# An eighth pair of split buffers in a float32 transformer kernel, and one more weight subunit ahead of the second half of the tokens

## The reference, cut to what matters

```python
for l in range(2):                                             # first_block
    h = h + 0.5 * rms_norm(swiglu(rms_norm(h, g[0]), ffn1_w_in[l], ffn1_w_out[l]), g[1])
    h = h + rms_norm(mixer(rms_norm(h, g[2])), g[3])           # even: attention and conv, odd: GLA
    h = h + 0.5 * rms_norm(swiglu(rms_norm(h, g[4]), ffn2_w_in[l], ffn2_w_out[l]), g[5])
mod = silu(c) @ w_ada + b_ada                                  # second_block: shifts, scales, gates
h = rms_norm(x, norm1_w) * (1 + scale1) + shift1
proj = h @ w_in                                                # 15 chunks of columns
x = x + gate1 * ((sigmoid(ga) * y_attention + sigmoid(gb) * y_retention) @ w_out)
h2 = rms_norm(x, norm2_w) * (1 + scale2) + shift2
x = x + gate2 * ((silu(h2 @ w_gate) * (h2 @ w_up)) @ w_down)
out = rms_norm(x, final_norm_w)
```

## Time and profile before

| | |
|---|---|
| median of 3 runs | 1436.91 us (1436.34 to 1437.31) |
| the profiled execution: its own time | 1435.01 us |
| its span, first to last instruction | 1433.2 us |
| mean granted TensorE clock over the span | 0.998 |
| PE busy | 1415.5 us of the span |
| DVE busy, ACT busy | 947.2 us, 719.7 us |

### The profile page before, as it was taken

The page is one execution under the profiler, slowest core; times in us unless marked ns, Lnnn a source line. Parts: engine busy times, 40 slices in busy tenths (PEclk is TensorE's granted clock), DMA queues, the critical chain, the costliest instruction groups (busy, mean ns, idle before and its releaser), DMA issues.

```text
span 1433.2 us, 18097 instructions
## 1 busy us (share of the span) xinstructions
PE 1415.5 (99%) x6819; PEld 1164.5 (81%) x6819; DVE 947.2 (66%) x1321; ACT 719.7 (50%) x1063; POOL 149.9 (10%) x237
## 2 busy tenths in 40 slices
PE   9999999999999999999999999999999999999997
PEld 7888888688888888888887888887877788788886
DVE  6666667877675667576796857755568566655543
ACT  6444465565443454444754635446556644654442
POOL 1600010010000000000261100001452110100000
PEclk9999999999999999999999999999999999999999
DMA  9586765167776777776643678873945355565551
GB/s 319 191 249 210 245 226 192 53 191 219 222 263 214 228 254 231 237 261 202 210 147 128 205 178 262 270 220 112 248 149 191 120 174 176 162 206 178 188 206 60
DMA packets 236342, 286.51 MB, mean 200 GB/s; under 512 B 37028, under 2 KB 160464, under 8 KB 236256
## 3 DMA queue, kind: packets, MB, share of 16 engines
q1 hardware_dynamic: 235856, 284.99, 62.4%
q10 hardware_dynamic: 400, 0.38, 0.1%
HBM read 281.13 MB, written 4.20 MB: 199 GB/s over the span
## 4 chain that ended last, share of the span: by engine, by line
PE 91%; DVE 4%; ACT 2%; issue 1%; DMA 1%; POOL 0%; POOLq 0%; ACTq 0%; DVEq 0%
PE ps L580 28%; PE ps L583 28%; PE ps L581 27%; PE ps L915 2%; DVE wlo L472 1%; DMA raw<-in_w_in_dram 1%; PE ps L776 1%; PE ps L1474 1%; PE ps L1175 1%; ACT whi L463 1%; PE ps L1122 0%; DVE h L1917 0%; DVE ps L1914 0%; PE ps L553 0%; PE ps L1059 0%
## 5 line engine op out<-in xcount | busy, mean ns | idle before, releaser
L472 DVE TENSOR_TENSOR wlo<-raw,whi 128x1024 fp32r<-128x1024 f32 (+2 forms) x474 | 564.9, 1225 | 248.6 <-ACT whi L463 248.2
L463 ACT ACTIVATE whi<-raw 128x1024 fp32r<-128x1024 f32 (+2 forms) x474 | 472.0, 1042 | 246.7 <-PE ps L583 94.0
L580 PE MATMUL ps<-whi,xh 128*128 128x512 f32 (+2 forms) x1438 | 566.3, 394 | 2.7 <-DVE wlo L472 1.7
L581 PE MATMUL ps<-wlo,xh 128*128 128x512 f32 (+2 forms) x1438 | 553.8, 385 | 0.0
L583 PE MATMUL ps<-whi,xl 128*128 128x512 f32 (+2 forms) x1438 | 545.9, 386 | 0.0
L580 PEld LDWEIGHTS ps<-whi,xh 128*128 128x128 f32 x1438 | 270.2, 188 | 60.6 <-DVE wlo L472 4.1
L583 PEld LDWEIGHTS ps<-whi,xl 128*128 128x128 f32 x1438 | 269.9, 188 | 55.2
L581 PEld LDWEIGHTS ps<-wlo,xh 128*128 128x128 f32 x1438 | 270.4, 188 | 50.6
L580 PE MATMUL ps<-whi,gh 128*128 128x512 f32 x440 | 172.6, 392 | 0.0
L581 PE MATMUL ps<-wlo,gh 128*128 128x512 f32 x440 | 171.3, 389 | 0.0
L583 PE MATMUL ps<-whi,gl 128*128 128x512 f32 x440 | 153.5, 389 | 0.0
(11 more groups left out here) (256 smaller groups left out, 900.0 us busy)
## 6 DMA issues: line engine op xcount, KB each, us to landing
raw<-in_ffn_w_in_dram SPq DMA_DIRECT2D x174, 512.0 KB, 5.5
raw<-in_ffn_w_out_dram SPq DMA_DIRECT2D x40, 1024.0 KB, 5.9
raw<-in_w_in_dram SPq DMA_DIRECT2D x26, 1024.0 KB, 5.1
adat<-in_w_ada_dram SPq DMA_DIRECT2D x96, 256.0 KB, 2.9
raw<-in_w_ffn_gate_dram SPq DMA_DIRECT2D x22, 512.0 KB, 4.0
raw<-in_w_ffn_up_dram SPq DMA_DIRECT2D x22, 512.0 KB, 5.1
raw<-in_hyb_w_in_dram SPq DMA_DIRECT2D x10, 1024.0 KB, 5.4
raw<-in_gla_w_in_dram SPq DMA_DIRECT2D x10, 1024.0 KB, 5.3
```

The costliest lines, as they stand in the source:

```text
L463: e.activation(split_of(whi, j), raw_of(j), ACT.Copy).then_inc(*whi_made.up(j))
L472: e.tensor_tensor(split_of(wlo, j), raw_of(j), split_of(whi, j).bitcast(F32), ALU.subtract).then_inc(*wlo_made.up(j))
L580: e.matmul(ps[:, 0:n], a, whi_of(j, k), start=first and k == 0, stop=False)
L581: last = e.matmul(ps[:, 0:n], a, wlo_of(j, k), start=False, stop=False)
```

## The change

The ring of split pairs gets an eighth slot, and the memory for it comes from buffers that are laid over others. `lrT` and `wg` (GLA's small gate operands, 16 partitions) now lie in `xtmp`; in stage 6 `pT` lies in the modulation's `adat`, `rt` in `adaacc`, `iw` and `ik2` in `fold`. The load of `wg` moves from unit 4 of stage 4 to behind unit 6, with a wait on `xlo_made`; ACT's copy to `lrT` gets a wait on `xlo_made`. `lead` grows by one in every stage but 0, and the calls that place the splits move with it. `LOOK` and `LAG` stay, and the place of the transposes of half 1 in `first_order`'s loop stays.

```diff
-NSPL = 7
+NSPL = 8
...
-            lead = {6: 7, 7: 7}.get(st, 6)
+            lead = {6: 8, 7: 8}.get(st, 7)
...
             act_h_squares(e, st, 0)
-            split_hi(e, j0 + 6)
+            split_hi(e, j0 + 7)
             act_enter(e, st, 1)
...
             split_lo(e, j0 + 6)
-            dve_enter(e, st, 1)
+            for q in range(2):
+                dve_gain(e, st, 1, q)
+            split_lo(e, j0 + 7)
+            for q in range(2):
+                dve_xlo(e, st, 1, q, xtmp_of(q))
             first(0)
...
                         e.wait_ge(*lr_turned.at())
+                        e.wait_ge(*xlo_made.at(4, 1, 1))
                         e.activation(lrT[:, :], tb.of("lr")[0:16, 0:256], ACT.Copy).then_inc(*lr_made.up())
...
             act_hn(e, st, 1)
+            split_hi(e, j0 + 8)
             act_ada_x(e, st, 1)
...
-            dve_ada_x(e, st, 1, lambda: split_lo(e, j0 + 7))
+            dve_ada_x(e, st, 1, lambda: split_lo(e, j0 + 8))
...
-                        e.wait_ge(*h_made.at(4, 1, 1))
-                        e.dma_start(wg[:, :], T["gla_w_gate"][0]).then_inc(*s_wg.up())
...
+                if u == U0[4] + 6:
+                    e.wait_ge(*xlo_made.at(4, 1, 0))
+                    e.dma_start(wg[:, :], T["gla_w_gate"][0]).then_inc(*s_wg.up())
```

More of the change, by code:

```diff
@@ L148, in program @@
         xtmp = sb("xtmp", 1024)
+        wg, lrT = xtmp[0:16, 0:512], xtmp[0:16, 512:768]
         mhalf = sb("mhalf", P)[:, 0:8]
@@ L413, in program @@
             lr = sb("glr", 32, where=inner)
-            lrT = sb("glrT", 256, where=inner, parts=16)
-            wg = sb("gwg", 512, where=inner, parts=16)
         with ExitStack() as inner:
@@ L418, in program @@
             AL = sb("AL", 1024, F32R, where=inner)
-            ar = sb("ar2", 13712, where=inner)
+            ar = sb("ar2", 11776, where=inner)
         def x_view(z, q, tok):
@@ L1969, in program @@
         sga, sgb = A(2048, 0), A(2048, 2048)
-        MB = A(384)
-        SCW = off[0]
-        SC, W = A(384), A(384)
+        MB, SC, W = A(384), A(384), A(384)
         PB = [SC, W, iqT[:, 0:384], iqT[:, 384:768]]
-        pT = [A(384), A(384)]
-        off[0] = SCW + 1536
-        RSb = A(1536, SCW)
+        off[0] = 4096 + 1536
+        RSb = A(1536, 4096)
         qrT, krT, vr, sgr = A(1024), A(1024), A(2048), A(2048)
-        rt = A(512)
         decay = hid[1][:, :]
-        iw, ik2 = A(16), A(256)
-        assert off[0] <= 13712, off[0]
+        assert off[0] == 11776, off[0]
+        pT = [adat[0][:, 0:384], adat[1][:, 0:384]]
+        rt = adaacc
+        iw, ik2 = fold[:, 0:16], fold[:, 256:512]
         MJ = {name: J0[6] + 4 * i for i, name in enumerate(
```

## The result

| | before | after |
|---|---|---|
| median | 1435.73 us (21 runs, 1434.86 to 1437.31) | 1438.24 us (21 runs, 1436.52 to 1442.29) |
| the profiled execution: own time, span | 1435.01, 1433.2 us | 1437.46, 1435.7 us |

The ratio of after to before is 1.0016, with a 95% interval from 1.0010 to 1.0022: 2.3 us slower (1.4 to 3.2). The forecast was 1.6 us. The two traces differ by 2.5 us of span, all of it in waits of PE.

What follows compares the result with a forecast made beforehand. PE, busy 1415.5 of 1433.2 us, was taken as the bound, so only its waits could change. Losses of 0.4 (stage 2), 0.3 (stage 4) and 0.9 (stage 6) make 1.6 us on 1436.91: 1438.5 us, range 1434.7 to 1441.6.

Steps and rivals of the forecast that it cites:

- no difference by 0.2%: Whole kernel: time changes by less than about 0.2%, which is 2.9 us; given a chance of 0.73.
- Stage 2, forecast 0.4: Opening of stage 2: a fifth split ahead of the residual starts it 1.8 us later; a loss of 0.4 us.
- Stage 4, forecast 0.3: Stage 4, narrow subunits: PE reaches (6, 0) before its `wlo` is ready; a loss of 0.3 us.
- Stage 1, forecast 0: Stage 1: `wlo` 6, made behind DVE's two L800, counted as ready when PE comes to (6, 0); 0 us.
- behind wider matmuls: Feed-forward stages and stage 1: PE comes to (6, 0) later, behind wider matmuls, so its `wlo` is ready; no loss.
- Stage 6, forecast 0.9: Inside stage 6: later half 1 delays casts, splits and loads, so PE's wait at L2398 grows from 0.9 to 1.8 us.
- so is every link: Stage 6: with (3, 1) 0.9 us later, every link of the chain to L2030 is 0.9 us later too.
- Rival C: Stage 6: the gate write also slows the load before it, landing 7.7 us late; 4.7 us slower, 1441.6 us; chance 0.16.
- The openings of stages 6 and 7, forecast 0: Openings of stages 6 and 7: PE's waits stand ahead of (0, 1), so the longer lead changes nothing; 0 us.
- list of waits at the openings: Openings of stages 2, 6 and 7: six waits of PE, 4.8 us in all.
- waits for PE there: Ends of most stages: DVE and ACT wait for PE, so one more split before the residual is free.
- Rival A: Stage openings: earlier splits shrink PE's waits by 2.0 or 4.8 us, to 1434.9 or 1432.1 us; chance 0.12.

Runs made afterwards that it cites:

- experiment 1: The change with `ahead` stopping one split earlier at the ends of stages, as before; eight slots and longer leads stay: ratio 1.0008 to the kernel before, span 1433.3 us.
- experiment 2: The change with only the end of stage 1 as before, one split earlier: ratio 1.0012 to the kernel before, span 1435.5 us.
- experiment 3: The change with the old leads and old split places; eight slots, memory and longer stage ends stay: ratio 1.0000 to the kernel before, span 1434.7 us.
- experiment 5: The kernel before with the second gate write moved from behind unit 8 to behind unit 29 of stage 6: ratio 0.9985, 2.2 us faster.
- experiment 6: The kernel before, seven slots, with one split less ahead of the residual at the end of stage 6: ratio 0.9988, span 1431.1 us.
- experiment 7: The change with `wlo` of subunit 6 made before DVE's four operations on half 1 in stages 6 and 7: ratio 1.0000 to the kernel before, span 1434.4 us.
- experiment 10: Eight slots, every lead and stage end as before, early `wlo` 6 in stages 6 and 7, gate write behind unit 29: 1431.29 us, 0.9962 to the kernel before.
- experiment 12: Eight slots, old stage ends, lead 8 in stages 6 and 7, early `wlo` 6, later gate write, plus a DVE pause in stage 7: 1430.83 us, 0.9963 to before.

## Why the prediction was right

**The size.** 1.6 us were forecast, the ratio gives 2.3 (1.4 to 3.2), and the sign and the class "no difference by 0.2%" held. That the sum came out is partly luck, since one term missed and another was only half understood. That the time came out to 0.3 us (1438.5 forecast, 1438.24 measured) is luck too: it was counted from a median of three runs, 1436.91 us, which lay 1.2 us above the median of all 21; from 1435.73 us the same 1.6 us lead to 1437.3.

**Stage 2, forecast 0.4, measured 0.5.** Shown by experiments 1 and 2. The working held to 0.1 us, down to the start of the residual.

**Stage 4, forecast 0.3, measured 0.2 at (6, 0).** It goes with the old leads (experiment 3).

**Stage 1, forecast 0, measured 0.3.** A miss. The step was that PE comes to the later half 1 "behind wider matmuls" and nothing waits; that was said of (6, 0), and I did not follow the evacuations of half 1 to L1063, the next transposes that need them. ACT's evacuation of half 1 (L1249 before, L1253 after) starts at 210.70 and 212.62: 1.92 us later, of which 0.56 are those of the first 10 us and 1.36 the six matmuls of the added subunit. Behind it stand six casts, and behind those four `wlo` on DVE and then the operation that makes the input of the transposes. DVE's timeline, before and after:

```profile
218.75 1.40 DVE L1341 SCALAR_TENSOR_TENSOR hid<-ps,st,hid 128x512 f32<-128x512 f32 x2
```

```profile
220.67 1.41 DVE L1345 SCALAR_TENSOR_TENSOR hid<-ps,st,hid 128x512 f32<-128x512 f32 x2
```

It ends 1.24 us ahead of L1059 before, and at 222.08 after, 0.14 us ahead of L1063. With the old leads L1059 follows without a gap again (experiment 3).

**Stage 6, forecast 0.9, measured 0.6.** The chain moves by 0.9 us, as traced link by link, and the gate write is behind the slow loads (experiment 5). But the step "so is every link" was too firm: the last link scatters between 12.9 and 14.4 us. Two kernels with eight slots and without the longer lead in stage 6 waited 1.25 and 1.61 us, and one with it 0.90 us (experiment 1), so the 0.6 us between two single traces is not shown to be the lead's. Rival C did not occur: the load ahead took 5.13 us. Whether the seven kernels with eight slots that kept the write in its place (0.90 to 2.33 us, the change among them) wait longer than those with seven (0.75 in the kernel before, no row in experiment 6) for a reason of their own stays open.

**The openings of stages 6 and 7, forecast 0, measured 0.** Right, and for the reason given: (6, 0) waited for a `wlo` that stood behind L1849, and moving that split took the two waits away (experiment 7). Even then the eighth subunit of half 0 earned nothing (experiment 10).

**What the prediction passed over.** Its list of waits at the openings leaves out two: 0.45 us for `wlo` at (3, 0) of stage 7 (1242.21) and 0.35 us at the opening of stage 6 (994.26). Neither changed (0.43 and 0.36 us after), so the sum did not suffer. It called the extra split at the ends of stages free wherever DVE "waits for PE there". It costs nothing against before, but it hides what the slot could give: 1.2 us at the opening of stage 7, where the residual stands behind a split that waits for its slot. Rival A, the shorter openings, was there to be had, by two edits of order that need no slot; the change made neither of them.

## What to carry to other kernels

Before a ring is made deeper, find the wait that its depth ends. Here a missing slot stood behind one wait of PE, at the opening of stage 7, and it went as well with seven slots by placing one split less; the eighth slot went to one more piece of work ahead of the critical one. In an in-order queue, look at what the instruction ahead of the critical one waits for: a split that is placed early but must wait for its slot holds up all behind it. And where a load takes more than twice its usual time, look for the small transfer issued next to it before tracing what waits for the load.

## What the runs showed of the hardware that was not expected

- A write of 1024 single floats to HBM (4 KB) takes 14.0 us in stage 6 of the kernel before and 13.2 us at its later place. Among closely following loads three of them take 12.3 to 13.6 us, where they take 5.1 to 6.6 us without it; among sparse ones the load issued 0.42 us ahead of it keeps its 5.1 us.
- POOL's operations on 128 x 1 elements go from 0.44 to 1.49 us and from 0.56 to 1.39 us while DVE runs two-input subtractions of 128 x 1024, and come back when DVE pauses (experiment 12).
- The first 10 us of the kernel differ by half a microsecond between executions of equal code, as much as the terms argued about here: PE's L641 starts at 8.23 us in the kernel before and at 8.63 and 8.84 us in experiments 5 and 6. A single trace of each side does not settle a term of that size, only the place of each wait.
